# Hyena filters with 128-row products and token halves on two partition halves

## What is computed

```python
h = jnp.sin(freq * (_hyena_pos_features(L) @ w1 + b1))     # 33 features, width 64
h = jnp.sin(freq * (h @ w2 + b2))
h = jnp.sin(freq * (h @ w3 + b3))
h = h @ w4                                                 # 64 x (2 orders, 2 directions, 512)
return h.reshape(L, ORDER, 2, D_HYENA) * decay[:, None, None, :]
```

## Time and profile before

| | us |
|---|---|
| median of 3 runs | 4341.66 (4341.53 to 4346.03) |
| profiled execution | 4359.5 |
| its span | 4357.7 |
| PE busy | 4161.8 (96%) |
| PE weight loads | 3124.3 (72%) |
| DVE busy | 2214.6 (51%) |
| ACT busy | 1455.4 (33%) |
| POOL busy | 104.7 (2%) |

### The profile page before, as it was taken

How to read it: one execution, slowest core, us unless ns; L and a number is a source line. 1 busy time by engine, 2 the same in 40 slices (tenths; PEclk the granted TensorE clock), 3 DMA queues, 4 the chain that set the end, 5 groups by cost and what they waited for, 6 DMA issues and landing times. The chain is left out here.

```text
span 4357.7 us, 47229 instructions
## 1 busy us (share of the span) xinstructions
PE 4161.8 (96%) x18868; PEld 3124.3 (72%) x18868; DVE 2214.6 (51%) x3340; ACT 1455.4 (33%) x2360; POOL 104.7 (2%) x158
## 2 busy tenths in 40 slices
PE   8988899999999999999999999989999999999997
PEld 3666665688888876665678888867777777887785
DVE  6686555553443345545553333354364554546656
ACT  2333445321121233344431211223344343324433
POOL 2100000000000000000000000000000000000000
PEclk6999999999999999999999999999999999999998
DMA  4432300033332120110012222121111111115541
GB/s 175 169 131 73 124 20 10 30 92 93 97 97 78 49 78 25 54 61 1 26 58 76 71 67 70 47 82 46 44 42 49 44 40 56 51 53 203 184 166 57
DMA packets 93666, 325.12 MB, mean 75 GB/s; under 512 B 10376, under 2 KB 11176, under 8 KB 92362
## 3 DMA queue, kind: packets, MB, share of 16 engines
q1 hardware_dynamic: 74874, 250.28, 17.5%
q0 software_dynamic: 18576, 71.84, 5.2%
HBM read 287.47 MB, written 34.60 MB: 74 GB/s over the span
## 5 line engine op out<-in xcount | busy, mean ns | idle before, releaser
L1014 PE MATMUL PS<-hi,WH 128*128 128x512 f32 x1440 | 569.4, 395 | 29.9 <-issue 13.4
L1014 PE MATMUL PS<-lo,WH 128*128 128x512 f32 x1440 | 568.0, 394 | 0.0
L1014 PE MATMUL PS<-hi,WL 128*128 128x512 f32 x1440 | 562.9, 391 | 0.0
L555 ACT ACTIVATE WH<-raw 128x1024 fp32r<-128x1024 f32 x304 | 319.8, 1052 | 663.2 <-PE PS L1014 504.9
L996 PE MATMUL PS<-hi,WH 128*128 128x512 f32 x1248 | 532.6, 427 | 1.7 <-ACT vf L1092 1.7
L996 PE MATMUL PS<-hi,WL 128*128 128x512 f32 x1248 | 493.7, 396 | 0.0
L996 PE MATMUL PS<-lo,WH 128*128 128x512 f32 x1248 | 492.0, 394 | 0.0
L565 DVE TENSOR_TENSOR WL<-raw,WH 128x1024 fp32r<-128x1024 f32 x264 | 322.8, 1223 | 186.5 <-ACT WH L555 186.3
L1014 PE MATMUL PS<-al,WH 128*128 128x512 f32 x1008 | 396.6, 393 | 0.0
L1014 PE MATMUL PS<-ah,WH 128*128 128x512 f32 x1008 | 395.7, 393 | 0.0
L1014 PE MATMUL PS<-ah,WL 128*128 128x512 f32 x1008 | 391.5, 388 | 0.0
(11 more groups left out here) (447 smaller groups left out, 6502.0 us busy)
## 6 DMA issues: line engine op xcount, KB each, us to landing
adab<-in_w_ada POOLq DMA_DIRECT2D x120, 512.0 KB, 4.6
raw<-in_win SPq DMA_DIRECT2D x104, 512.0 KB, 3.6
raw<-in_up SPq DMA_DIRECT2D x64, 512.0 KB, 3.6
raw<-in_down SPq DMA_DIRECT2D x64, 512.0 KB, 3.6
raw<-in_dft SPq DMA_DIRECT2D x24, 512.0 KB, 4.0
sp_x<-X SPq DMA_DIRECT2D x24, 512.0 KB, 5.3
X<-sp_x SPq DMA_DIRECT2D x24, 512.0 KB, 5.8
raw<-in_wout SPq DMA_DIRECT2D x24, 512.0 KB, 3.7
```

The costliest lines, as they stand in the source:

```text
L555: act.activation(WH[:, j % 2, :], raw[:, j % 2, :], ACT.Copy).then_inc(*W_HI.next(j))
L1014: mm = pe.matmul(bank[b + hf], w[:, k, :], r[:, k, HALF[hf]], start=k == 0 and w is wh and r is hi, stop=k == 7 and w is wl)
```

## The change

The tokens' halves are put on partitions 0 to 63 and 64 to 127, so layers one and two take one round of 128 partitions each; layer three is done per half of the tokens with its output twice, on both halves of the partitions. Of that, `hst` holds the high part (fp32r) in rows 0 to 63 and the low part in rows 64 to 127. `w4` is loaded twice, on both halves; its sum and difference move from POOL to DVE and are split as well (`wph`, `wpl`). A filter product is then `hst` x `wph` plus `hst` x `wpl`, two fp32r products of 128 rows. Tiles alternate between banks 6, 7 and 4, 5. ACT copies the even banks of a spectrum after its fourth group rather than after its eighth. The angle's reduction loses two steps, a sine early on loads ACT's table, the mask arrives as bytes, and the planned times are moved.

```diff
@@ -117,13 +117,13 @@
-FILTERS = 45.0
+FILTERS = 23.0
 def filter_tick(cs, m, nt):
...
 def layer_at(l):
-    return 190.0 + 1238.5 * l
+    return 143.0 + 1238.5 * l
@@ -260,7 +260,7 @@
 def ada_plan():
-    q = [(0, 8 * (j % 2) + j // 2, FILTERS + 5 + 6.5 * j) for j in range(16)]
+    q = [(0, 8 * (j % 2) + j // 2, FILTERS + 6 + 6.3 * j) for j in range(16)]
@@ -294,19 +294,26 @@
-        self.col = sb(top, "col", [P, 2])
+        self.col = sb(top, "col", [P, 3])
...
-            self.h3 = sb(c, "h3", [64, S])
-            self.w4 = sb(c, "w4", [64, 2, 2, HS])
-            self.wpm = sb(c, "wpm", [64, 2, 2, HS])
+            self.hst = sb(c, "hst", [P, S], R)
+            self.wph = sb(c, "wph", [P, 2, 2, HS], R)
+            self.wpl = sb(c, "wpl", [P, 2, 2, HS], R)
...
+                self.h12 = sb(c2, "h12", [P, HS])
+                self.h3 = sb(c2, "h3", [P, S])
...
-                self.fw23 = sb(c2, "fw23", [64, 2, 64])
-                self.fred = sb(c2, "fred", [64, 2, S])
-                self.lmf = sb(c2, "lmf", [P, 8, P])
+                self.fw2 = sb(c2, "fw2", [P, 64])
+                self.fw3 = sb(c2, "fw3", [P, P])
+                self.fred = sb(c2, "fred", [P, 2, S])
...
+                sb(c2, "gap1", [P, 25, P * 2])
+                self.w4 = sb(c2, "w4", [P, 2, 2, HS])
+                self.wpm = sb(c2, "wpm", [P, 2, 2, HS])
@@ -528,7 +535,7 @@
         def split_time(j):
-            return (WEIGHTS[j - 1][1] if j else 0.0) + 1
+            return WEIGHTS[j - 1][1] + 1 if j else 14.6
@@ -625,13 +632,13 @@
-            sp.dma_start(m.fw23[:, 0, :], D["fw2"]).then_inc(*FE_IN.next(0, by=16))
-            sp.dma_start(m.fw23[:, 1, :], D["fw3"]).then_inc(*FE_IN.next(0, by=16))
+            sp.dma_start(m.fw2[:, :], D["fw2"]).then_inc(*FE_IN.next(0, by=16))
+            sp.dma_start(m.fw3[:, :], D["fw3"]).then_inc(*FE_IN.next(0, by=16))
...
-            sp.dma_start(m.lmf[:, :, :], D["lmask"]).then_inc(*LM_IN.next(0, by=16))
+            sp.dma_start(m.lmask[:, :, :], D["lmask"]).then_inc(*LM_IN.next(0, by=16))
@@ -640,33 +647,73 @@
         def setup_pool(pool):
...
-            pool.wait_ge(*W4_IN[0])
-            for o in range(2):
-                pool.tensor_tensor(m.wpm[:, 0, o, :], m.w4[:, o, 0, :], m.w4[:, o, 1, :], ALU.add)
-                pool.tensor_tensor(m.wpm[:, 1, o, :], m.w4[:, o, 0, :], m.w4[:, o, 1, :],
-                                   ALU.subtract).then_inc(*WPM.next(o))
+        def feature_line(dve, x, b, i, k):
+            dve.tensor_scalar(x, b, vc("fb", i), vc("ffreq"), ALU.add, ALU.mult).then_inc(*DVE_OWN.next())
+            dve.wait_ge(*DVE_OWN.now())
+            dve.tensor_scalar(k, x, INV2PI, MAGIC, ALU.mult, ALU.add).then_inc(*DVE_OWN.next())
+            dve.wait_ge(*DVE_OWN.now())
+            dve.tensor_scalar(k, k, -MAGIC, None, ALU.add).then_inc(*FE_DVE.next("turns", i))
+        def feature_angle(dve, event, x, k, r):
+            dve.wait_ge(*FE_DVE.now())
+            for n, c in enumerate((C1, C2, C3)):
+                dve.scalar_tensor_tensor(out=r, in0=k, scalar=-c, in1=r if n else x, op0=ALU.mult,
+                                         op1=ALU.add).then_inc(*DVE_OWN.next())
+                dve.wait_ge(*DVE_OWN.now())
+            dve.tensor_scalar(r, r, PI, -PI, ALU.min, ALU.max).then_inc(*FE_DVE.next("angle", *event))
         def setup_dve(dve):
...
-            for i in range(3):
-                for hf in range(2):
-                    yield 6 + 12.0 * i + 6 * hf
-                    h, k, r = m.h3[:, HALF[hf]], m.fred[:, 0, HALF[hf]], m.fred[:, 1, HALF[hf]]
-                    dve.wait_ge(*FE_PE[i, hf])
-                    dve.tensor_scalar(h, PS[0:64, hf, :], vc("fb", i, R64), vc("ffreq", 0, R64), ALU.add,
-                                      ALU.mult).then_inc(*FE_DVE.next("line", i, hf))
-                    dve.wait_ge(*FE_DVE.now())
-                    reduce_angle(dve, DVE_OWN, h, k, r, False)
-                    dve.wait_ge(*DVE_OWN.now())
-                    dve.tensor_scalar(r, r, -PI, None, ALU.max).then_inc(*FE_DVE.next("angle", i, hf))
-            yield 9.0
+            k, r = m.fred[:, 0, :], m.fred[:, 1, :]
+            for i in range(2):
+                yield 8.0 + 7 * i
+                dve.wait_ge(*FE_PE[i])
+                feature_line(dve, m.h12[:, :], bank[i], i, k[:, HALF[0]])
+                feature_angle(dve, (i,), m.h12[:, :], k[:, HALF[0]], r[:, HALF[0]])
+            for hf in range(2):
+                yield 22.0 + 4.4 * hf
+                dve.wait_ge(*FE_PE[2, hf])
+                feature_line(dve, m.h3[:, HALF[hf]], bank[2 + hf], 2, k[:, HALF[hf]])
+                if hf:
+                    feature_low(dve, 0)
+                feature_angle(dve, (2, hf), m.h3[:, HALF[hf]], k[:, HALF[hf]], r[:, HALF[hf]])
+            yield 32.4
+            feature_low(dve, 1)
+        def feature_low(dve, hf):
+            rows = slice(64, P)
+            dve.wait_ge(*FE_ACT["high", hf])
+            dve.tensor_tensor(m.hst[rows, HALF[hf]], m.h3[rows, HALF[hf]], m.hst[rows, HALF[hf]].bitcast(F),
+                              ALU.subtract).then_inc(*FE_DVE.next("low", hf))
+        def setup_cond_dve(dve):
+            yield 14.0
...
-            dve.wait_ge(*LM_IN[0])
-            dve.tensor_copy(m.lmask[:, :, :], m.lmf[:, :, :]).then_inc(*LM.next(0))
+        def setup_weights_dve(dve):
+            for cs in range(2):
+                yield 13.0 + 8 * cs
+                if cs == 0:
+                    dve.wait_ge(*W4_IN[0])
+                for o in range(2):
+                    dve.tensor_tensor(m.wpm[:, cs, o, :], m.w4[:, o, 0, :], m.w4[:, o, 1, :],
+                                      ALU.subtract if cs else ALU.add).then_inc(*WPM.next("sum", cs, o))
+            for cs in range(2):
+                yield (21.5, 38.9)[cs]
+                for o in range(2):
+                    dve.wait_ge(*FE_ACT["weights", cs, o])
+                    dve.tensor_tensor(m.wpl[:, cs, o, :], m.wpm[:, cs, o, :], m.wph[:, cs, o, :].bitcast(F),
+                                      ALU.subtract).then_inc(*WPM.next("low", cs, o))
@@ -686,53 +733,80 @@
-            for i in range(3):
-                for hf in range(2):
-                    yield 12 + 12.0 * i + 6 * hf
-                    act.wait_ge(*FE_DVE["angle", i, hf])
-                    act.activation(m.h3[:, HALF[hf]], m.fred[:, 1, HALF[hf]], ACT.Sin,
-                                   bias=0.0).then_inc(*FE_ACT.next(i, hf))
+            act.wait_ge(*COL[0])
+            act.activation(m.col[:, 2:3], t_eps, ACT.Sin, bias=0.0)
+            for i in range(2):
+                yield 12.0 + 7 * i
+                act.wait_ge(*FE_DVE["angle", i])
+                act.activation(m.h12[:, :], m.fred[:, 1, 0:HS], ACT.Sin, bias=0.0).then_inc(*FE_ACT.next(i))
+            for hf in range(2):
+                yield 26.5 + 4.4 * hf
+                act.wait_ge(*FE_DVE["angle", 2, hf])
+                act.activation(m.h3[:, HALF[hf]], m.fred[:, 1, HALF[hf]], ACT.Sin, bias=0.0).then_inc(*FE_ACT.next(2, hf))
+                act.wait_ge(*FE_ACT[2, hf])
+                act.activation(m.hst[:, HALF[hf]], m.h3[:, HALF[hf]], ACT.Copy).then_inc(*FE_ACT.next("high", hf))
+        def setup_weights_act(act):
+            for cs in range(2):
+                yield (15.0, 22.5)[cs]
+                for o in range(2):
+                    act.wait_ge(*WPM["sum", cs, o])
+                    act.activation(m.wph[:, cs, o, :], m.wpm[:, cs, o, :], ACT.Copy).then_inc(*FE_ACT.next("weights", cs, o))
         def setup_pe(pe):
...
+            rows = [slice(0, 64), slice(64, P)]
...
-            spare_pe(pe, 7, 3, early)
+            spare_pe(pe, 7, 4, early)
...
-            for i in range(3):
-                for hf in range(2):
-                    yield 5 + 12.0 * i + 6 * hf
-                    if i:
-                        spare_pe(pe, 7, (4, 0, 1, 1)[2 * i - 2 + hf], early)
-                        pe.wait_ge(*FE_ACT[i - 1, hf])
-                    pe.matmul(PS[0:64, hf, :], m.fw23[:, i - 1, :] if i else m.fw1[:, :],
-                              m.h3[:, HALF[hf]] if i else m.feat[:, HALF[hf]],
-                              start=True, stop=True).then_inc(*FE_PE.next(i, hf))
+            for hf in range(2):
+                mm = pe.matmul(PS[rows[hf], 0, :], m.fw1[:, :], m.feat[:, HALF[hf]], start=True, stop=True)
+            mm.then_inc(*FE_PE.next(0))
+            spare_pe(pe, 7, 5, early)
+            yield 13.0
+            pe.wait_ge(*FE_ACT[0])
+            for hf in range(2):
+                mm = pe.matmul(PS[rows[hf], 1, :], m.fw2[rows[hf], :], m.h12[rows[hf], :], start=True, stop=True)
+            mm.then_inc(*FE_PE.next(1))
+            spare_pe(pe, 7, 5, early)
+            yield 20.5
+            pe.wait_ge(*FE_ACT[1])
+            for hf in range(2):
+                pe.matmul(bank[2 + hf], m.fw3[rows[hf], :], m.h12[rows[hf], :], start=True, stop=True).then_inc(
```

(42 more changed lines are left out.)

12 lines of the change are left out of this document (7 added, 5 removed).

## The result

| | before | changed |
|---|---|---|
| median of the runs, us | 4341.59 (4341.12 to 4346.03, 4 runs) | 4311.17 (4310.19 to 4312.37, 4 runs) |
| ratio of the times | | 0.9928, 95% interval 0.9911 to 0.9945 |
| profiled execution, us | 4359.5 | 4310.71 |
| its span, us | 4357.7 | 4308.9 |
| logarithm of the first norm, us | 203.70 | 159.29 |

The changed kernel is faster, by 30.4 us between the medians and by 48.8 between the two profiled executions. The forecast was 48 and 4293.7, with 4307 as the upper end of its range: the gain in the runs is more than a third smaller than forecast.

What follows compares the result with a forecast made beforehand. PE bounds the kernel after 213 us and is unchanged there, so only the norm's start moves: 29.6 won by the end of (0,0), 33.9 by (0,3), 43.3, 47.7, then 0.6 of tail: 48 off 4341.66 gives 4293.7, range 4285 to 4307.

Steps and rivals of the forecast that it cites:

- the last one of the sum: Whole kernel: the 48 us gained are subtracted from the median of the runs, 4341.66, not from the profiled execution, giving 4293.7.
- the 18 us: Profiled execution of the kernel before, 4359.5, stood 18 us above the median; claimed to lie past the norm or in the launch.
- Network: Feature network at the start: four rounds replace six, so the first filter product starts at 32.1 us against 43.04.
- a wait at L709: Feature network: DVE waits there for w4, landing at 15.7 us, bounds 14.7 and 17.3.
- The rival of late transfers: Early loads: POOL's 1 MB delays w4 to 17.3 or later; gain 44 to 46.4, 4296.5 in the middle; chance 0.07.
- First values: Between network and filter loop: `ft` starts at 35.95 and the first `hl` comes at 41.7 us against 50.85.
- Filter loop: Loop with spectrum (0,0): clock rises at 50, then DVE sets the pace; it ends at 65.0 us against 94.6.
- The mis-sized term: Filter loop on DVE: low parts at 0.68 us each, eight lows and fourteen values together 15.2.
- Dense spectra: After the loop: the 1.27 gap goes, spectra start 11.0 us apart, and (0,3) starts at 86.9 against 120.84.
- What I had named as a sign of being wrong: Second filter loop: DVE's work between 100 and 115 us stops PE for more than 1 us.
- (0,3) and (1,0): The two spectra with the later filter steps: 30.0 us against 39.4, bringing the gain to 43.3.
- Norm: Start of the first RMS norm, its logarithm: at 155.4 us for 203.7, 48 us less, nothing gained behind it.

## Why the prediction was wrong, point by point

**The step that failed is the last one of the sum:** "that difference lies past the norm or in the launch, so I subtract from the median". It does not. The profiled execution of before was one of the slowest of its kernel (4359.5, where 64 runs reach from 4335.5 to 4359.8), and the repeat of the same kernel shows where: 13.35 of the 15.3 us between the two are in the filter loop at 0.50, from whose 43.7 us (first `hl` to the end of (0,0)) the sum had just taken 20. The changed kernel does not have that stretch, and its clock was back at 46 us, so this part of the 18 us was counted twice. The median of three runs was a low base as well: 64 later runs have 4346.2. Against its own execution the total came out, partly by luck (point 6): 4359.5 - 48 = 4311.5, and 4310.71 was measured. Or from the other side: the repeat's norm stood at 190.35 and its time at 4344.21, so the forecast norm of 155.4 saves 35 and gives 4309. A rise of the clock at 91 us after 47 us at the lower level was in the earlier trace rows; that it need not be the same in every run I did not ask, although a profiled time 18 us above three runs was there to ask it.

The steps themselves, from the profiled execution of before to that of the changed kernel:

1. *Network.* First filter product 31.00, forecast 32.1. (The 5.25 us of a round before are nine steps of DVE, not eleven; the sum used the 5.25 and two steps less, and is not changed by it.) w4 did not decide (forecast: landed at 15.7, a wait at L709). It was the small `fw` that came late, 9.70 for 7.8, and everything behind it had its own length. The rival of late transfers was right about the mechanism and wrong about the victim; holding POOL's loads gave back 1.9 us here, and the rest of the 3.4 at the norm was the clock. The Trainium skill (DMA: Bandwidth & Descriptors, "Issuing engines are not separate DMA queues") says that loads from all queues share the engines; the trace agrees, with a DMA share of 1.02 for 0.48 at 4 to 6 us.
2. *First values.* First `hl` at 40.31, forecast 41.7.
3. *Filter loop.* Clock up at 46 rather than 50, and DVE sets the pace, as forecast. But the loop took 3.1 us longer than the sum: (0,0) ended at 66.7 instead of 65.0 from a start that was 1.4 earlier. The mis-sized term is the low part, 0.68 in the sum: eight of them took 9.8 us for 5.4, because four of them stood beside POOL's (1.74 to 1.78). The trace of before had this to read: two of its eight took 1.74 and 1.76, and POOL's last one, beside a dot, 2.12. From the first `hl` to the end of DVE's last it was 22.6 for 20.1 (values a little shorter than in the sum gave back the rest), and 0.6 more came from POOL's last one, 2.31 beside a dot where I had 1.3 to 1.5. The Trainium skill (SBUF — State Buffer, "SBUF: two separate sides") describes the pair of ports that DVE and POOL share as an exclusive lock under which the later one fully blocks; the trace agrees: POOL's `hl` ran from 42.92 to 44.19, DVE's from 42.97 to 44.74, which is the end of POOL's and 0.55 more, where one alone takes 0.69. The values `ft`, with one input in PSUM, kept their 0.68 beside POOL's low part (46.65 and 47.25, POOL from 46.68 to 47.99).
4. *Dense spectra.* 11.20 apart for 11.0, and (0,1) 12.75, since the clock was down from 66 to 70. Six profiles of the changed kernel and its variants have two idle stretches of more than 1 us there. In four of them the clock fell beside them (this one, the one with one pair of banks and the two with spare products). In the other two it did not: with the loads held, behind stretches of 2.22 and 2.69, and with the late copy, behind 2.03 and 2.68. With the dots moved, where the stretches are at most 0.9, it did not fall either. So the stretches alone do not decide it, and what does is open. PE's waits behind a full DVE were in none of my steps. (0,3) started at 90.7 for 86.9. What I had named as a sign of being wrong, DVE stopping PE between 100 and 115, did not happen: PE had no idle time there.
5. *(0,3) and (1,0)* took 29.5, forecast 30.0; three more spectra 33.6, forecast 33.0.
6. *Norm* at 159.29, forecast 155.4, so 44.4 were won here and not 48. The rest of the 48.8 between the two profiles, 4.4, lies behind the norm, where I had forecast nothing. It cannot be told from chance: that stretch differed by up to 7 us over the profiles, by the windows above through falls of the clock that come and go. That the total agreed to 1 us is therefore partly luck.

**What each part brought.** Five stretches divide the way to the norm; "three parts" is the kernel before with the copy, the banks and the spare products:

| us | before | before, repeated | three parts | changed | forecast |
|---|---|---|---|---|---|
| to the first `hl` | 50.85 | 50.76 | 50.57 | 40.31 | 41.7 |
| from there to the start of (0,1) | 44.97 | 31.72 | 25.43 | 26.42 | 23.3 |
| (0,1) and (0,2) | 25.02 | 25.01 | 21.97 | 23.95 | 21.9 |
| (0,3) and (1,0) | 40.66 | 40.67 | 39.15 | 29.53 | 30.0 |
| from there to the norm | 42.20 | 42.19 | 38.43 | 39.08 | 38.5 |

Of the 31.1 us between the repeat and the changed kernel the network is 10.4, and the early copy 8.5 to 8.8 by its own two runs. The second pair of banks is worth about 5 together with the 128-row products, and without them nothing at the lower clock and perhaps 2.3 at 1.00. The 128-row products gain in the second filter loop, (0,3) and (1,0), where PE has no idle time at a clock of 1.00: 9.6 us less than in the kernel with the three parts. In the first loop they show no gain over that kernel, whose spare products keep the clock at 1.00 there: DVE is full in the changed kernel, which takes 1.0 longer. Together with 2.6 in the stretches of dense spectra (the fall at 66 and the slower groups) this makes the 6.0. A changed kernel with f32 products was not tried.

## What to carry to other kernels

A profiled execution that stands far above the median of the runs has probably lost the difference somewhere in its own trace: repeat it, look for the place, first in stretches at the lower clock, before a gain is subtracted from the median, and above all if the change removes such a stretch. When a change makes DVE the bound of a loop, take everything off it that can wait, also small work that an order placed there while DVE had room: here the sixteen dot products moved behind the loop brought 5.7 us at the norm (155.90 to 150.17), beside the 31 of the whole change. Operations of DVE and POOL that both read two operands from SBUF are to be costed one after the other where they meet, as the low parts here.

## What was not expected of the hardware

- The clock in the same program, with starts alike to 0.1 us from 22 us on, came back at 62 us in one execution and at 91 in the first, and at 69 in one of the kernel with other banks; the 29 us of delay cost 13.4. With seven more spare products around the pair of one-row products it stayed at 1.00 from 40 to 90. The Trainium skill (TensorE: Matmul & The Clock Gate, "A second HAM failure mode: psum-queue depth-cycling") tells of a clock that goes back and forth with short idle spells of PE between groups; the fall at 66 behind two idle stretches of 2.34 and 2.69 us fits that, but two executions with nearly the same stretches had no fall, and the low stretch of before, in which PE showed no idle time from 60 to 86, does not fit it.
- Short falls of the clock, some 7 us each, come and go at the same places behind the norm from one execution to the next (0.59 and 0.57 for 1.00 in the two windows above).
- In the changed kernel's profile, and in that with the held loads, a group of six fp32r products took 1.40 us in the dense spectra at a granted clock of 1.00 (11.20 / 8), in the profiles with spare products or moved dots mostly 1.37 (10.98 / 8), and with one pair of banks first the one and then the other. It is 0.2 us for a spectrum, and its cause is open.
